# Head loads in 64-row pieces, bias-table transfers moved on the SyncE queue, and high parts of keys and queries written by ScalarE from PSUM

## The reference, cut to what matters

```python
q, k, v, xr, gr = jnp.split(hl @ w_in, splits, axis=-1)
kc, vc = heads(hc @ w_k), heads(hc @ w_v)
att = neighbourhood_attention(heads(q), heads(k), heads(v), kc, vc, rpb)
xr = dwconv(xr, conv_w, LRU_PAD) + conv_b
rec, rec_c = bidir_rglru(xr, xc, lru_wr, lru_br, lru_wi, lru_bi, lru_lam, ctx_out)
y = jnp.concatenate([att, rec * jax.nn.gelu(gr)], axis=-1) @ w_out
```

## Time and profile before

| | before |
|---|---|
| median of 3 runs | 2368.63 us (2362.93 to 2369.1) |
| the profiled execution's own time | 2365.85 us |
| its span | 2364.0 us |
| PE busy | 2255.5 us (95%) |
| DVE, POOL, ACT busy | 1493.1, 1221.4, 817.9 us |
| granted PE clock, mean | 0.98 |
| DMA mean | 120 GB/s |

### The profile page before, as it was taken

How to read it: one execution, slowest core, us unless ns; L and a number is a source line. 1 busy time by engine, 2 the same in 40 slices (tenths; PEclk the granted TensorE clock), 3 DMA queues, 4 the chain that set the end, 5 groups by cost and what they waited for, 6 DMA issues and landing times.

```text
span 2364.0 us, 27340 instructions
## 1 busy us (share of the span) xinstructions
PE 2255.5 (95%) x10278; PEld 1842.5 (78%) x10278; DVE 1493.1 (63%) x1895; ACT 817.9 (35%) x1359; POOL 1221.4 (52%) x765
## 2 busy tenths in 40 slices
PE   8998997788989999999999989999999999999998
PEld 3787786677868888888888867888778888888887
DVE  5587772564387555556777798665875555555553
ACT  4434443674343222323122532232633233332122
POOL 3365641469846555556445236565355555565440
PEclk9998998899999999999999999999999999999999
DMA  8665455553412222227565022243123222243322
GB/s 313 197 177 141 139 172 146 137 130 126 121 49 94 88 91 85 81 81 267 195 224 182 26 59 77 77 161 92 32 89 99 81 80 81 80 152 107 107 72 80
DMA packets 296702, 282.95 MB, mean 120 GB/s; under 512 B 64543, under 2 KB 241915, under 8 KB 296059
## 3 DMA queue, kind: packets, MB, share of 16 engines
q1 hardware_dynamic: 258507, 257.61, 34.6%
q10 hardware_dynamic: 37488, 21.50, 3.1%
q0 software_dynamic: 576, 2.10, 0.2%
HBM read 226.36 MB, written 57.16 MB: 120 GB/s over the span
## 4 chain that ended last, share of the span: by engine, by line
PE 76%; DVE 11%; DMA 5%; issue 3%; ACT 2%; POOL 2%; SPq 1%; ACTq 0%; DVEq 0%; POOLq 0%
PE bank L1104 24%; PE bank L1106 24%; PE bank L1105 24%; DMA q_st<-q_spill 2%; DVE mod_acc_p L2402 1%; PE bank L1185 1%; DVE x_conv L2390 1%; DVE act_lo L2091 1%; DMA q_spill<-qk_raw 1%; DVE act_hi L2091 1%; DMA bias_t<-rpb_full 1%; PE bank L1313 1%; PE bank L1139 0%; DVE lru_q L2417 0%; SPq L715 0%
## 5 line engine op out<-in xcount | busy, mean ns | idle before, releaser
L2010 DVE SCALAR_TENSOR_TENSOR h<-bank,mods,h 128x512 f32<-128x512 f32 x384 | 287.7, 750 | 272.0 <-PE bank L1106 266.7
L1065 POOL TENSOR_TENSOR slot_lo<-pair_raw,slot_hi 128x512 fp32r<-128x512 f32 x112 | 170.7, 1524 | 286.3 <-ACT slot_hi L1602 286.3
L1065 POOL TENSOR_TENSOR slot_lo<-t_sum,slot_hi 128x512 fp32r<-128x512 f32 x109 | 166.9, 1553 | 153.2 <-ACT slot_hi L1602 153.2
L1065 POOL TENSOR_TENSOR slot<-pair_raw,slot 128x512 fp32r<-128x512 f32 x144 | 231.1, 1626 | 16.0 <-ACT slot L1602 16.0
L2171 DVE TENSOR_TENSOR bank<-bank,p 128x512 f32<-128x512 f32 x53 | 37.0, 698 | 287.2 <-PE bank L1106 287.1
L1104 PE MATMUL bank<-act_lo,slot_hi 128*128 128x512 f32 x436 | 170.8, 392 | 6.6 <-DVE act_lo L2091 5.9
L1104 PE MATMUL bank<-a,slot_hi 128*128 128x512 f32 x436 | 171.7, 394 | 2.5 <-ACT p L1611 0.8
L1602 ACT CAST slot_hi<-pair_raw 128x512 fp32r<-128x512 f32 x112 | 69.1, 617 | 293.8 <-DMA pair_raw<-in_ffn_w_gu 245.4
L1106 PE MATMUL bank<-a,slot_hi 128*128 128x512 f32 x436 | 170.5, 391 | 0.0
L1106 PE MATMUL bank<-act_lo,slot_hi 128*128 128x512 f32 x436 | 170.0, 390 | 0.0
L1105 PE MATMUL bank<-a,slot_lo 128*128 128x512 f32 x436 | 169.7, 389 | 0.0
(11 more groups left out here) (318 smaller groups left out, 6082.4 us busy)
## 6 DMA issues: line engine op xcount, KB each, us to landing
pair_raw<-in_ffn_w_gu SPq DMA_DIRECT2D x88, 512.0 KB, 4.4
mod_in_f<-in_mod_w SPq DMA_DIRECT2D x48, 512.0 KB, 3.7
z_spill<-silu_g SPq DMA_DIRECT2D x88, 256.0 KB, 2.2
mod_in_p<-in_mod_w SPq DMA_DIRECT2D x32, 512.0 KB, 5.9
pair_raw<-in_o_w_in SPq DMA_DIRECT2D x24, 512.0 KB, 3.7
raw<-in_e_w_in SPq DMA_DIRECT2D x20, 512.0 KB, 4.6
low_f<-z_spill SPq DMA_DIRECT2D x40, 256.0 KB, 5.1
a_f<-z_spill SPq DMA_DIRECT2D x18, 512.0 KB, 6.1
```

The source lines that it names most:

```text
L1065: nc.gpsimd.tensor_tensor(low, from_, high, ALU.subtract).then_inc(s_wlo, 1)
L2010: V.scalar_tensor_tensor(out=dst, in0=bank[:, b, :], scalar=mods[:, gate, m:m + 1], in1=dst, op0=ALU.mult, op1=ALU.add).then_inc(s_hup, 1)
```

## The change

- `load_head`: the one transfer of `q_st` becomes two of 64 rows. `kl` is loaded to rows 0 to 63 alone. Five transfers remain.
- `scores`: the matmul against `kl` takes rows 0 to 63 of both operands (query high by key low); the product low by low is left out.
- The bias transfers move down on SP's queue. `fill_bias` goes behind the fourth weight unit of round 1, `widen_bias` to the same place of round 2, the first half of `place_bias` to that of round 3, and the second half behind the second value unit.
- `qk_hi` is made by ACT from the PSUM bank, right before `qk_raw`, with the waits for `s_qh` and for the low part of piece n - 2. `split_piece` on POOL keeps the subtraction alone. `store_piece` is called twice: the high part's store right behind its making, the low part's where both stood.

```diff
@@ sync: round i
-                if i == 1:
-                    fill_bias()
-                    widen_bias()
-                else:
-                    place_bias(range(ROWS // 2 * (i - 2), ROWS // 2 * (i - 1)))
...
                 load_unit(4 * i + 3, 1, column_unit(w_in, i * P + order_p[3]))
+                if i == 1:
+                    fill_bias()
+                elif i == 2:
+                    widen_bias()
+                else:
+                    place_bias(range(ROWS // 2))
                 sp.wait_ge(s_gate, i * 12)
                 load_gates(i)
...
                     for k in range(4, FT):
                         load_mod_p(LT - 2, k)
+                    place_bias(range(ROWS // 2, ROWS))
@@ load_head
-                    sp.dma_start(kl[half, :], k_spill[1, pair, own, :]).then_inc(s_head[head % 2], 16)
-                sp.dma_start(qs, q_spill[:, pair, own, :]).then_inc(s_head[head % 2], 16)
+                    sp.dma_start(qs[half, :], q_spill[a, pair, own, :]).then_inc(s_head[head % 2], 16)
+                sp.dma_start(kl[0:64, :], k_spill[1, pair, own, :]).then_inc(s_head[head % 2], 16)
@@ gpsimd: split_piece
-                if n >= 2:
-                    pool.wait_ge(s_qh[n % 2], X_DONE + 16 * (n // 2))
-                nc.gpsimd.tensor_tensor(qk_hi[:, n % 2, 0:w], qk_raw[:, n % 3, 0:w], ones[:, 0:1].to_broadcast([P, w]),
-                                        ALU.mult).then_inc(s_qkh, 1)
@@ tensor: scores
-                    mm = pe.matmul(out_, q, kl[:, part], start=False, stop=True)
+                    mm = pe.matmul(out_, q[0:64, :], kl[0:64, part], start=False, stop=True)
@@ scalar: round i
+                    if n >= 2:
+                        act.wait_ge(s_qh[n % 2], X_DONE + 16 * (n // 2))
+                        act.wait_ge(s_qkl, n - 1)
                     if n >= 3:
                         act.wait_ge(s_ql[n % 3], X_DONE + 16 * (n // 3))
                     if part < 2:
-                        nc.scalar.activation(by_blocks(qk_raw[:, n % 3, :]), by_rows(bank[:, g % 5, :]), ACT.Copy,
-                                             scale=-(64 ** -0.5) if unit == 1 else 1.0).then_inc(s_projev, 1)
+                        scale = -(64 ** -0.5) if unit == 1 else 1.0
+                        nc.scalar.activation(by_blocks(qk_hi[:, n % 2, :]), by_rows(bank[:, g % 5, :]), ACT.Copy, scale=scale).then_inc(s_qkh, 1)
+                        nc.scalar.activation(by_blocks(qk_raw[:, n % 3, :]), by_rows(bank[:, g % 5, :]), ACT.Copy, scale=scale).then_inc(s_projev, 1)
                     else:
+                        nc.scalar.copy(qk_hi[:, n % 2, 0:w], bank[:, g % 5, 0:w]).then_inc(s_qkh, 1)
                         nc.scalar.copy(qk_raw[:, n % 3, 0:w], bank[:, g % 5, 0:w]).then_inc(s_projev, 1)
+                    store_piece(i, piece, 0)
                     if piece >= 2:
-                        store_piece(i, piece - 2)
+                        store_piece(i, piece - 2, 1)
```

More of the change, by code:

```diff
@@ L1813, in out_of, with store_piece @@
                     act.wait_ge(s_proj, 10 * i + g + 1)
-                def store_piece(i, x):
+                def store_piece(i, x, a):
                     n, (unit, part) = 5 * i + x, GROUPS[PIECES[x]]
                     w = CTX if part == 2 else HALF
[L1819 to L1826, removed]
+                    if a:
+                        act.wait_ge(s_qkl, n + 1)
+                        tile, done = qk_raw[:, n % 3, 0:w], s_ql[n % 3]
+                    else:
+                        act.wait_ge(s_qkh, n + 1)
+                        tile, done = qk_hi[:, n % 2, 0:w].bitcast(F32), s_qh[n % 2]
+                    if part < 2:
+                        dst = q_spill[a, i] if unit == 1 else k_spill[a, i, :, CTX:]
+                        act.dma_start(dst.rearrange("p (j h n) -> h p j n", j=TT, h=2)[part],
+                                      tile.rearrange("p (j n) -> p j n", j=TT)).then_inc(done, 16)
+                    else:
+                        act.dma_start(k_spill[a, i, :, 0:CTX], tile).then_inc(done, 16)
                 act.wait_ge(s_conv, i + 1)
@@ L1857, in _ @@
                                          ACT.Gelu_apprx_tanh).then_inc(s_projev, 1)
-                    store_piece(i, g - 5)
+                    store_piece(i, g - 5, 1)
                 for g in range(12):
```

## The result

| | before | changed |
|---|---|---|
| median of 5 runs each, in turns | 2365.63 us (2362.93 to 2369.1) | 2354.94 us (2349.51 to 2357.43) |
| ratio, 95% interval | | 0.9948 (0.9932 to 0.9965) |
| the profiled execution: time, span | 2365.85, 2364.0 us | 2354.94, 2353.1 us |

The change makes the kernel faster by 11 us, not by 59. The sign is right; the time is 22 us above the end of the range.

A forecast was written before the change was run, and what follows sets the result against it. PE bounds the kernel (76% of the chain), with idle time before `gates(i)` and late attention loads to gain. Projection 21.0 plus attention 38 makes 59 us: 2368.6 - 59 = 2309 us, range 2295 to 2333.

The forecast's parts named there:

- The load of `q_st` in two pieces: Attention: spreading the query's load hides every load but head 1's; gain 33 to 44 us, taken as 38.
- `kl` on 64 rows: Attention `scores`: saved bytes are hidden, and turns between 128 and 64 rows were taken to cost 0.
- the dear end: Rival, `scores`: each 128/64-row turn empties PE, 0.16 us each, 41 us, 2351 us, 5 in 100; doubled, 2391 us, 3 in 100.
- `gates(1)`: Projection: earlier weight splits and less POOL work bring DVE in time; PE's 8.93 us wait goes, 6.0 without POOL's relief.
- `gates(0)`: Projection: with `fill_bias` moved, stores land sooner and PE's 5.76 us wait is gained.
- the ACT part: Projection: making high parts on ACT gains nothing there; its new waits cost 0 to 2 us a round, inside slack.
- the projection keeps its waits: Rival, projection: stores on ACT's queue stay slow and ACT late; 3 of the 21 us come, 2327 us, 14 in 100.
- `gates(2)`: Projection: DVE's time falls from 53.1 to 48.3 us, under PE's 50.1, so PE's 2.94 us wait goes.
- `gates(3)`: Projection: ACT stays late through a store of 10.25 us, so PE's 2.36 us wait stays.
- the tail: End of the attention: unchanged, PE still waits 5.84 us for POOL.
- the moved `widen_bias` and `place_bias`: SP's queue: some 11 us of issuing each, hidden; the bias table is complete some 70 us before it is read.
- The lower clock behind `gates(0)`: Projection: PE's slower work behind the wait at `gates(0)` goes with that wait; gain 3.4 us.

The follow-up runs named there:

- e3: The kernel before with one edit: `q_st` loaded by two transfers of 64 rows instead of one; 2328.0 us, ratio 0.9834.
- e1: The changed kernel with the matmul against `kl` on all 128 rows again and `kl` loaded to both halves; 2309.29 us, ratio 0.9757.
- e9: The changed kernel itself, measured and profiled once more; 2350.62 us, ratio 0.9939.
- e8: e7 with two of ACT's four copies of the recurrence's high parts three steps later; 2299.27 us, ratio 0.971.
- e2: The changed kernel with the `scores` matmuls reordered, both against `kh` first, then both against `kl`: two turns a step, not four; 2322.52 us, ratio 0.9812.
- e10: e1 with the matmul against `kl` on rows 0 to 95 of both operands; 2311.81 us, ratio 0.9768.
- e4: The kernel before with the matmul against `kl` on rows 0 to 63 alone, loads as before; 2372.19 us, ratio 1.0028.
- e5: The kernel before with the bias transfers alone moved to their new places on SP's queue; 2356.6 us, ratio 0.9956.
- e7: e1 with the first four rows of modulation weights (2 MB) issued behind unit 7 instead of ahead of unit 4; 2303.46 us, ratio 0.9732.

## Why the prediction was right or wrong, step by step

**The load of `q_st` in two pieces: right.** Expected 33 to 44 us; e3 gives 39 alone, and e1 131.8 us from first to last logits against 131. That the total fits so closely is in part luck, since two errors cancel: the heads of e1 sum to 115.6 us instead of 8 x 13.63 = 109.0 (head 6 alone takes 18.0), and the seven changes of head to 16.3 instead of 21.4.

**`kl` on 64 rows, "so I take 0": this step failed.** The kernel gained 11 us instead of 59; this step is 38.9 of the 48 missing (36.1 by the profile of e9). Between the changed kernel and e1 the stage differs by 170.72 - 131.81 = 38.9 us:

- the turns in heads 2 to 5 and 7: 90.2 - 69.8 = 20.5 us, 4.1 a head;
- the same in heads 0 and 1, at 4.1: 8.2 us;
- what is left of heads 0 and 1, put down to the lower clock: 44.48 - 27.79 - 8.2 = 8.5 us (5.7 in e9);
- changes of head: 17.9 - 16.3 = 1.6 us;
- head 6: 0.1, as its 18 us in e1 come from ACT's wait, which e8 takes out.

The row that I chose, eight transposes over 2 rows ahead of a matmul over 128, was the wrong neighbour: I read one turn off a modelled end (47.24) and one start (47.17), in a stretch where PE had other reasons to be late. A transpose over 2 rows may or may not have been in another mode; the row couldn't tell. The other end, 0.16 us a turn from rows 14, was nearly exact: the heads grew by 0.15 a turn, and PE's rows by 0.17. That its total of 41 us lies so near 38.9 is partly luck: about 29 us are turns, the rest goes with the lower clock, which that rival didn't have. With ends of 0 and 41 us from rows, the range should have reached 2351; it ended at 2333, since I gave the dear end 5 in 100. The Trainium skill, "TensorEngine Tiling (Array Packing)", section "Key Properties", says that a change of tiling mode drains TensorE. The times of e1 and e2 agree with that for 64 rows beside 128 (0.13 to 0.17 us a turn), and e10 shows no such cost for 96 beside 128; no row of a trace names the mode itself.

**The clock, not in the sum at all.** I had counted on less of the lower clock in the attention, since no wait was left. In before, heads 0 and 1 took 13.69 and 13.97 us. In each kernel here the clock falls to 0.50 within 3 us of the first logits. Windows of 2 us give its start and its end, for the changed kernel and for e1:

```profile
368.00:370.00 2.00, 1.06 (x4) 0.66 (x3) 0.70 (x2) 1.39 (x2) 0.00 (x0) 0.86 0.39 118
...
402.00:404.00 2.00, 2.00 (x7) 1.10 (x5) 0.17 (x1) 0.86 (x3) 0.00 (x0) 0.60 1.05 409
```

```profile
362.00:364.00 2.00, 1.07 (x6) 0.87 (x5) 0.83 (x2) 1.87 (x4) 0.00 (x0) 0.62 0.22 82
...
368.00:370.00 2.00, 2.00 (x11) 1.63 (x9) 1.08 (x4) 1.50 (x3) 1.51 (x1) 0.67 1.03 220
```

In between it is 0.50. That makes 34 us at the lower clock in the changed kernel and 7 in e1; read in the same way this first stretch is 27 in e9 and in e4, 20 in e2, and 3 in e10, in e3 and in before (which has further ones behind its waits for loads). So the long stretch comes with the turns and is shorter with fewer of them, although PE is marked busy in nearly all of it: 23.1 of the 24 us from 372 to 396 in the changed kernel. Why it lasts as long as it does, and why it differs between two profiles of one kernel, no run isolates.

**`gates(1)`: right.** Its 8.93 us of idle time and the lower clock behind it went, 11.3 us in all; units 6 and 7 were split by 120 us, ahead of the recurrence. e5 alone leaves 2.87 us of the 8.93, the 6.0 foreseen.

**`gates(0)`: mis-sized by a step of the ACT part, "nothing" for its new waits.** The bias part alone gives 4.3 of 5.76 (e5). What I had left out is that the store of a high part has to land before ACT may write the ring buffer again, and that it lands no faster than the low part's. From the timeline of ACT in the changed kernel:

```profile
95.29 0.60 ACT L1847 ACTIVATE qk_hi<-bank 128x512 fp32r<-128x512 f32 x1 [6.75 <-DMA q_spill<-qk_hi]
...
101.40 0.60 ACT L1847 ACTIVATE qk_hi<-bank 128x512 fp32r<-128x512 f32 x1 [5.02 <-DMA q_spill<-qk_raw]
...
108.36 0.37 ACT L1850 CAST qk_hi<-bank 128x256 fp32r<-128x256 f32 x1 [5.88 <-POOL qk_raw L966]
```

The first row is a wait for a buffer that in before POOL stood in, off the path; the next two follow from it. `xc_hi` is queued behind them, and PE waits 7.26 us at `gates(0)`, where a gain of 5.76 was forecast. The prediction allowed 0 to 2 us and looked at rounds 1 and 2 alone. The rival "the projection keeps its waits" was right for this one of the four places.

**`gates(2)`: right in mechanism, short in size, and it varies.** DVE was to be freed from 53.1 to 48.3 us. It took 52.9 (239.59 - 186.71) in the first profile, 50.4 in e9 and 50.0 in e1. POOL's relief is partly given back, since its weight splits now lie beside the start of the recurrence, whose instruction takes 2.40 us there and took 1.49. Of the 2.5 us between the two profiles of one kernel, 1.7 are a single row at the end. DVE and POOL of the changed kernel, first profile:

```profile
236.50 1.91 POOL L940 TENSOR_TENSOR w_hi<-raw,ones 128x1024 fp32r<-128x1024 f32 x1 [6.62 <-DMA r_spill<-lru_q]
...
236.57 2.92 DVE L2448 TENSOR_TENSOR xc_lo<-x_conv,xc_hi 128x1024 fp32r<-128x1024 f32 x1
```

and DVE in e9:

```profile
234.67 1.22 DVE L2448 TENSOR_TENSOR xc_lo<-x_conv,xc_hi 128x1024 fp32r<-128x1024 f32 x1
```

The last low part, for which PE waits, takes 2.92 us when POOL's next split begins beside it and 1.22 when not. PE idles 2.77 us at `gates(2)` in the one and 0.28 in the other.

**`gates(3)`, the tail, the moved `widen_bias` and `place_bias`: right.** 2.13 us of idle time against 2.36, and nothing waited for the bias table.

**The lower clock behind `gates(0)`**, 3.4 us, didn't come, as the wait didn't go in the changed kernel. In e7, where the idle time at `gates(0)` went from the 7.32 us of e1 to 0.80, `gates(0)` comes 6.5 us earlier, and from `gates(0)` to `gates(1)` it takes 58.0 us instead of 59.8. So the clock gives at most 1.8 us there, about half of the 3.4.

In sum: attention -1.5 instead of +38 us (+1.3 in e9), projection +14.3 instead of +21 (up to +19.9 in the other profiles with this projection, so that the 21 is short by 1 to 7 us), and 1.7 us of start that belongs to no edit.

## What to carry to other kernels

In a chain where each step waits for PE's last, don't let matmuls over 64 rows alternate with matmuls over 128 (96 beside 128 did no harm here); if a 64-row operand is needed, order the matmuls so that the row count turns as seldom as it can, and price each turn before counting saved bytes. Read the outermost size of both sides of each DMA: a 2 there cost 39 us, and one small edit mends it. When a cost has no row of its own, an end of the bounds that the nearest like rows give (0.28 long, 0.12 apart) is worth more than one unlike row that seems to say zero. A handover to another engine takes its ring-buffer waits along: look what is queued behind them there.

## What the runs showed of the hardware that was not expected

- A turn between 128 and 64 rows costs PE 0.13 to 0.17 us at the full clock (1.37, 0.97 and 0.71 us for the same four matmuls with four, two and no turns). Between 128 and 96 rows it costs nothing (282 and 284 ns).
- PE's busy time as the page counts it contains these turns, and the lower clock: it rose by 33.5 us when matmuls got smaller. A busy share of 12.00 in 12 us is no sign of useful work.
- A granted clock of 0.50, the lower of the two levels, held for 27 to 34 us while PE was marked busy nearly throughout, in both profiles of the changed kernel and in e4, for 20 us with two turns a step, and for 3 to 7 at the same point of the kernels without 64-row matmuls. The four matmuls of `scores` with their four turns take 2.25 us at this level (382.86 to 385.11 us in the changed kernel), against 1.27 to 1.37 at the full clock.
- The two halves of a change can hide each other: 64 rows cost 5 us on slow loads and 41 to 46 on quick ones.
